# The order of small work at the seam between layers: map transposes, channel copies and squares in a two-block kernel

## What is computed

```python
x = x + gate * (concatenate([rw_l, mla_l]) @ w_out)       # end of the first block
x = rms_norm(x, final_g)
for layer in range(2):                                    # second block
    xn = rms_norm_2(h, attn_norm_g[layer])
    proj = xn @ w_in[layer]
    u_ssm, u_g, v_g, q, k, v = split(proj)
    y_ssm  = s5_mixer(u_ssm, ...)                         # state space, 1024 states
    y_sgu  = spatial_gating(u_g, v_g, gmlp_w_s, ...)      # 128x128 maps over positions
    y_diff = diff_attention(q, k, v, ...)
    h = h + concatenate([y_ssm, y_sgu, y_diff]) @ w_out[layer]
    xn = rms_norm_2(h, ffn_norm_g[layer])
    h = h + conv_gated_mlp(xn, w_up, conv_w, conv_b, w_down)
```

## Time and profile before

| | us |
|---|---|
| median of 3 runs | 1208.89 |
| the three runs | 1209.45, 1202.99, 1208.89 |
| the profiled execution | 1204.26 |
| its span | 1202.3 |
| mean granted clock of TensorE in it | 0.968 of full speed |

### The profile page before, as it was taken

One profiled execution on the slowest core, in us unless ns is written; L12 is line 12 of the kernel. 1 busy time (PEld: TensorE's weight loads), 2 busy tenths in 40 slices (PEclk: granted clock), 3 DMA queues, 4 the chain that ended last, 5 costly groups with the idle time before them and its releaser, 6 DMA issues.

```text
span 1202.3 us, 15594 instructions
## 1 busy us (share of the span) xinstructions
PE 1138.0 (95%) x6191; PEld 793.6 (66%) x6191; DVE 645.4 (54%) x1360; ACT 337.5 (28%) x786; POOL 113.0 (9%) x107
## 2 busy tenths in 40 slices
PE   5899999979779999999999999999999999999998
PEld 2444858657778696546478888644556488888543
DVE  3222315768797964798326566630698236566400
ACT  2212223766444233324121211200525111211100
POOL 0000101110120011162000000010261000000000
PEclk9799999999787987999999999999999999999999
DMA  9722332000003202642238543334442264444400
GB/s 356 267 71 73 125 140 75 1 1 1 2 1 99 89 19 70 226 167 97 70 102 255 169 149 140 141 118 141 161 140 71 72 208 140 141 146 175 170 35 35
DMA packets 96665, 140.05 MB, mean 116 GB/s; under 512 B 12207, under 2 KB 63058, under 8 KB 96466
## 3 DMA queue, kind: packets, MB, share of 16 engines
q1 hardware_dynamic: 96228, 138.94, 34.1%
q10 hardware_dynamic: 366, 0.13, 0.0%
HBM read 138.01 MB, written 1.05 MB: 116 GB/s over the span
## 4 chain that ended last, share of the span: by engine, by line
PE 76%; DVE 17%; ACT 3%; DMA 2%; issue 2%; POOL 0%; SPq 0%; DVEq 0%; ACTq 0%
PE bank L1335 25%; PE bank L1354 13%; PE bank L825 12%; PE bank L480 2%; PE bank L473 2%; DMA ring<-in_ada_w 2%; PE bank L1163 2%; DVE work L2590 2%; PE bank L1097 1%; DVE work L2585 1%; PE bank L619 1%; PE bank L1153 1%; PE bank L1044 1%; DVE rot L2570 1%; DVE work L2583 1%
## 5 line engine op out<-in xcount | busy, mean ns | idle before, releaser
L1335 PE MATMUL bank<-work,ring 128*128 128x256 f32 x1024 | 222.7, 379 | 0.0
L1335 PEld LDWEIGHTS bank<-work,ring 128*128 128x128 f32 x1024 | 194.2, 190 | 26.2
L825 PE MATMUL bank<-work,ring 128*128 128x256 f32 (+1 forms) x432 | 140.5, 484 | 2.3 <-ACT work L1405 2.3
L1354 PE MATMUL bank<-ring,work 128*128 128x512 f32 x288 | 124.3, 592 | 0.0
L825 PEld LDWEIGHTS bank<-work,ring 128*128 128x128 f32 x432 | 82.5, 194 | 55.8 <-issue 49.3
L1853 ACT ACTIVATE work<-work,prm 128x256 f32<-128x256 f32 x88 | 48.0, 592 | 250.5 <-DVE work L2730 224.0
L1354 PEld LDWEIGHTS bank<-ring,work 128*128 128x128 f32 x288 | 54.7, 190 | 68.0 <-issue 67.4
L2722 DVE TENSOR_TENSOR work<-bank,turned 128x512 f32<-128x512 f32 x44 | 30.4, 692 | 112.0 <-PE bank L1335 111.9
L1335 PE MATMUL bank<-work 128*128 128x256 f32 x384 | 83.9, 379 | 0.0
L1335 PEld LDWEIGHTS bank<-work 128*128 128x128 f32 x384 | 73.0, 190 | 9.9
L2740 DVE SCALAR_TENSOR_TENSOR work<-work,prm 128x256 f32<-128x256 f32 x176 | 77.1, 480 | 4.2 <-ACT work L1853 2.6
(11 more groups left out here) (454 smaller groups left out, 1779.2 us busy)
## 6 DMA issues: line engine op xcount, KB each, us to landing
ring<-in_w_up SPq DMA_DIRECT2D x32, 1024.0 KB, 7.7
ring<-in_w_in SPq DMA_DIRECT2D x24, 1024.0 KB, 7.4
ring<-in_w_down SPq DMA_DIRECT2D x16, 1024.0 KB, 6.1
ring<-in_ada_w SPq DMA_DIRECT2D x12, 1024.0 KB, 11.2
work<-in_w_up SPq DMA_DIRECT2D x12, 1024.0 KB, 7.7
ring<-in_w_out SPq DMA_DIRECT2D x10, 1024.0 KB, 6.1
work<-in_w_in SPq DMA_DIRECT2D x4, 1024.0 KB, 8.4
work<-in_w_down SPq DMA_DIRECT2D x4, 1024.0 KB, 6.0
```

Source lines behind the costliest of these rows:

```text
L825: ins = mm(b[0:rows, 0:toks], wt[:, k, off:off + rows], hT[:, k, 0:toks], start=(k == 0), stop=(k == KD - 1))
L1335: ins = mm(b[:, SEQ * half:SEQ * half + SEQ], wt[:, KD * half + k, P * j:P * j + P], xnT[:, k, :], start=(k == 0), stop=(k == KD - 1))
L1354: ins = mm(acc[2 * t + j][:, :], actT[:, k, P * t:P * t + P], wt[:, q, 512 * j:512 * j + 512], start=(k == 0), stop=(k == FB - 1))
```

## The change

Nothing is computed differently; only orders change. TensorE turns the maps between the two halves of the rows instead of ahead of them, for both layers. ScalarE copies bank 0 of the rows ahead of its last squares (ahead of the fourth pair into layer 0, ahead of the third of four squares into layer 1) and bank 2 ahead of the maps. VectorE copies bank 1 ahead of `wsT` and bank 3 after it.

```diff
-                def to_channels(key, x, ready):
+                def to_channels(key, x, ready, between=None):
                     for j in range(4):
+                        if j == 2 and between:
+                            between()
                         if j % 2 == 0:
                             pe.wait_ge(*ready(j // 2))
...
-                pe.wait_ge(S["p2_load"], 16 * P2_DMAS * (l + 1))
-                pe.wait_ge(*turn(("wsT", l)))
...
+                def small_maps():
+                    pe.wait_ge(S["p2_load"], 16 * P2_DMAS * (l + 1))
+                    pe.wait_ge(*turn(("wsT", l)))
...
                 if l:
-                    to_channels("xa", xc, lambda j: when_empty(("down", l - 1, 2 + j)))
+                    to_channels("xa", xc, lambda j: when_empty(("down", l - 1, 2 + j)), small_maps)
                 else:
-                    to_channels("xa", xs2, lambda j: (S["z_f"], 2 * j + 2))
+                    to_channels("xa", xs2, lambda j: (S["z_f"], 2 * j + 2), small_maps)
...
             for j in range(2):
                 for t in range(2):
                     cols, q = slice(512 * j, 512 * j + 512), 2 * j + t
+                    if q == 3:
+                        channels_even(0, "xa", "attn_g", 0)
                     act.wait_ge(S["x1"], q + 1)
...
                     for q in range(4):
+                        if q == 2:
+                            channels_even(l, "xa", "attn_g", 0)
                         square_sum(2 * l, q, when_empty(("down", l - 1, 2 * (q % 2) + q // 2)))
+                channels_even(l, "xa", "attn_g", 2)
                 take_maps()
-                channels_even("xa", "attn_g", 0)
-                channels_even("xa", "attn_g", 2)
...
-                def channels_odd(key, gain):
-                    for j in range(1, 4, 2):
+                def channels_odd(key, gain, js=(1, 3)):
+                    for j in js:
...
+                channels_odd("xa", "attn_g", (1,))
                 take_mixing()
-                channels_odd("xa", "attn_g")
+                channels_odd("xa", "attn_g", (3,))
```

More of the change, by code:

```diff
@@ L1131, in _ @@
-                for c in range(2):
-                    for j in range(2):
[L1133 to L1140, removed]
@@ L1141, in _ @@
-                ins.then_inc(*filling(("bT", l)))
+                def small_maps():
+                    pe.wait_ge(S["p2_load"], 16 * P2_DMAS * (l + 1))
+                    pe.wait_ge(*turn(("wsT", l)))
+                    b = bank_of(("wsT", l))
+                    for h in range(4):
+                        ins = tr(b[:, P * h:P * h + P], ws[:, h, :], ident)
+                    ins.then_inc(*filling(("wsT", l)))
+                    pe.wait_ge(S["c_masked"], l + 1)
+                    pe.wait_ge(*turn(("cT", l)))
+                    b = bank_of(("cT", l))
+                    for c in range(2):
+                        for j in range(2):
+                            ins = tr(b[:, (2 * c + j) * P:(2 * c + j + 1) * P], c_rows[:, c, j, :], ident)
+                    ins.then_inc(*filling(("cT", l)))
+                    pe.wait_ge(S["b_spread"], l + 1)
+                    pe.wait_ge(*turn(("bT", l)))
+                    b = bank_of(("bT", l))
+                    for j in range(2):
+                        for c in range(2):
+                            ins = tr(b[:, (2 * j + c) * P:(2 * j + c + 1) * P], bexp[:, j, c].rearrange("p a b -> p (a b)"), ident)
+                    ins.then_inc(*filling(("bT", l)))
@@ L1687, in state_tables, with channels_even @@
                 A.activation(csc[:, :, 1, :], ang, ACT.Sin, bias=small[:, 383:384], scale=-TWO_PI).then_inc(S["tables"], 1)
+            def channels_even(l, key, gain, j):
+                act.wait_ge(*when_full((key, l, j)))
+                b = bank_of((key, l, j))
+                for i in range(2):
+                    k = 2 * j + i
+                    ins = A.activation(xnT[:, k, :], b[:, SEQ * i:SEQ * i + SEQ], ACT.Copy, scale=k2(l, gain, 1, k))
+                ins.then_inc(*emptying((key, l, j)))
             act.wait_ge(S["mix_rw"], 2)
@@ L1721, in square_sum @@
                                  accum_out=small[:, 336 + q:337 + q]).then_inc(S["ssq_a"], 1)
[L1723 to L1729, removed]
                 if l:
@@ L1840, in _ @@
                     square_sum(2 * l + 1, q, when_empty(("out2", l, q // 2, q % 2)))
-                channels_even("xf", "ffn_g", 0)
+                channels_even(l, "xf", "ffn_g", 0)
                 square_sum(2 * l + 1, 3, when_empty(("out2", l, 1, 1)))
-                channels_even("xf", "ffn_g", 2)
+                channels_even(l, "xf", "ffn_g", 2)
                 def gelu_part(m):
```

## The result

The changed kernel took 1200.07 us (median of 18 runs, 1198.03 to 1205.57), the kernel before 1208.2 us (18 runs, 1201.49 to 1210.76): a ratio of 0.9944, with a 95% interval of 0.9931 to 0.9958. By the interval that is 5.1 to 8.3 us less, where the sum said 3.4. The profiled execution took 1199.53 us with a span of 1197.6, 4.7 us less than the one of before.

A forecast was written before the change was run, and what follows sets the result against it. TensorE's first product at both seams was taken to wait for ScalarE's last row copies; 2.3 us (layer 0) + 1.1 us (layer 1) = 3.4 us off the median of 1208.9 gives 1205.5 us, range 1199.3 to 1209.0.

The forecast's parts named there:

- the sum: Both seams together: 2.3 + 1.1 = 3.4 us off the kernel, 0.28%.
- What bounds the seams: At both seams TensorE's first product waits for ScalarE's last two row copies: 1.90 us into layer 0, 1.12 into layer 1.
- Layer 0, 2.3 us: Seam into layer 0: the first product starts at 489.92 instead of 492.21, a gain of 2.3 us.
- tight place: Layer 0: factors ready 0.05 us before their product L1120 is due; time VectorE's five copies lose comes off one for one.
- Layer 1, 1.1 us: Seam into layer 1: the first product starts at 845.97 instead of 847.09, a gain of 1.1 us.
- The squares' wait: Layer 1: ScalarE waits for bank 0 before two squares, done at 845.73 against 844.63; 1.2 us are free.
- 0.5 us later tables: Layer 1: ScalarE's four tables end at about 855.8 instead of 855.25; hidden by 2.4 us.
- Costs of nothing: Layer 0: bank 0's copy hides in ScalarE's wait, the weights' transfer is hidden by 3.5 us, the maps' users are far off.
- By these rows there is no clock to win or lose: Both seams: the granted clock was 1.00 despite TensorE's idle 1.90 and 1.12 us, so no clock gain or loss.
- likeliest case: Whole kernel: the 3.4 us forecast with the median where it was, 1205.5 us, own range 1204.5 to 1207.9; chance 0.60.
- rival D: Whole kernel: same mechanism, but the median falls on the scatter's low side, 1199.6 us, 0.8% faster; chance 0.25.
- Rival C: Clock falls to 0.50 behind the seams: 3.69 us more on the product, about 7.6 per seam, 1220.7 at both; chance 0.03.

The follow-up runs named there:

- e8: The changed kernel with VectorE's product that takes the wsT bank done twice at both seams; 1200.93 us, one execution.
- e2: The changed kernel with the new order only at the seam into layer 1, the old order into layer 0; 1207.89 us, ratio 1.0007 to before.
- e3: The changed kernel with TensorE's new order alone, the copies on ScalarE and VectorE in the old order; 1209.68 us, one execution.
- e4: The changed kernel with the copies' new order on ScalarE and VectorE alone, TensorE in the old order (maps first); 1205.64 us, one execution.
- e0_before_again: The kernel of before, unchanged, run again; 1209.53 us, ratio 1.0022 to other runs of the same kernel.
- e0_after_again: The changed kernel, unchanged, run again; 1200.39 us, ratio 0.9963 to before.
- e10: The kernel of before, unchanged, run a third time, on the same chip as e9 and e11; 1209.2 us, ratio 0.9998.
- e11: The changed kernel, unchanged, run a third time, on the same chip as e9 and e10; 1200.95 us, ratio 0.9939 to before.
- e1: The changed kernel with the new order only at the seam into layer 0, the old order into layer 1; 1204.04 us, ratio 0.9973 to before.
- e5: The kernel of before with 16 and 8 identity transposes filling TensorE's wait at the seams; 1207.02 us, ratio 1.0008 to before.
- e7: The changed kernel with head tables built in VectorE's wait and the scan's first inputs made ahead of the query rows; 1201.28 us, ratio 0.995 to before.
- e9: e7 with the second pair of scan inputs also ahead of the query rows' second group; 1201.65 us, ratio 0.9944 to before.

## Why the prediction was right, and where it fell short

- **What bounds the seams:** right. ScalarE's order held the first product; the product starts directly behind the transposes.
- **Layer 0, 2.3 us:** 2.25 measured in every trace. The factors as the tight place: shown by e8, one for one.
- **Layer 1, 1.1 us:** 1.2 measured: the product starts 1.13 us earlier and takes 3.62 us instead of 3.69. The squares' wait and the 0.5 us later tables were there and cost nothing.
- **Costs of nothing:** ScalarE's copy of bank 0 in its wait, the weights' transfer, the maps behind the copies: no wait for any of them in the trace of the changed kernel.
- **The sum:** 3.4 us, 3.45 in the traces, but 5.1 to 8.3 in the times. The step that fell short is "By these rows there is no clock to win or lose". It rested on one execution of before. In e2, e3 and e4 the product behind TensorE's idle time ran mostly at the lower level and took 1.69 us more each. The Trainium skill (TensorE: Matmul & The Clock Gate, HAM oscillation) says that gaps between bursts bring the clock down; it tells it of waits for transfers that are longer than these gaps. Those three traces are in line with it for gaps of 0.8 to 2.4 us, and the traces of before, where 0.78 and 1.90 us passed at 1.00, show that it doesn't happen each time. I had quoted the rule and given it no chance in the kernel of before.
- **The predicted time:** 1205.5 predicted, 1200.07 measured, outside the likeliest case's own 1204.5 to 1207.9. It lies in the range only because the range was stretched to rival D's 1199.6; that the total fell inside is luck, the seams are not.
- **Rival D**, more than the sum by luck of the median, had the right time (1199.6), but luck is not the whole reason: more than the sum came back twice, with medians 9.1 us apart (e0_before_again, e0_after_again) and 8.3 us (e10, e11). Some of it is luck: against the 35 other executions of before on the first chip it is 5.1 us, and over all executions the means are 5.8 apart.
- **Rival C** named the mechanism, a fall of the clock at a seam, but not its price or the kernel: it put 3.69 us more on one product and 7.6 on a seam, and a fall cost 1.69 us, since the lower level ended within the product; and it was seen with the old order or half of it, never with the new.
- **Open:** no profiled execution of before has a mean clock under 0.968, so where the slowest of them lose their 5 us is not seen. The first product's 1.7 us can be part of it, but not all. No trace has a granted clock under 1.00 between 500 us and the seam into layer 1; ahead of L1097 all have some, and how much the slowest executions have there was not seen. The table shows that the loss goes away with the new order, and e1 against e2 that it hangs mainly on the seam into layer 0. That idle time causes it is argued, not shown: e5 filled part of the idle time, and its times did not fall.

## What to carry to other kernels

Split a copy queue so that what the next product needs comes ahead of what is needed later, and move the producer's order with it: where PSUM banks are handed out in program order, either half alone made waits through the ring. Give TensorE's idle time a chance of costing more than its length, since the product after it may run at the lower clock (1.69 us in e2, e3 and e4), and look at more than one execution before ruling that out. When a seam's gain is a few us in a kernel that scatters by nine, read it between anchors in the trace.

## What the runs showed of the hardware that was not expected

The same program on the same idle gaps was granted the full clock in three traces of before and 0.58 over 3.5 us behind them in e2; the clock fell behind idle time in e3 and e4 as well. In all eight traces where L1097 took 15.67 us instead of 13.97, its first part ran slow (in the profile of before the clock was granted at 0.67 from 472 to 475 us and at 1.00 from 475 on), and the product behind layer 0's seam was at full clock. Where it took 13.97, the product was slow in the two kernels whose gap was as long as before or longer (e2, e3), and not in the four whose gap was shorter or partly filled (e1, e5, e7, e9). But in three of these four the lower level lasted until about 1 us before L1097 instead (0.50 from 463 to 473 us in e1 and e7, to 472.5 in e5). Only e9 had neither: 0.50 from 464 to 470.5 us, then 1.00 from 471 to 487 and over the product. So that the order of work decides whether a fall hits the product rests on one clean trace against two, and is a guess.
